# Hybrid decoder step on one core: row splits, memory queries, W_out scaling and the loads of expert chunks 3 to 5 in another order

## What is computed

```
z = rmsnorm(x) @ w_in                     # 1024 -> 1792
q, k, v, cb, cc, cv, mq = split(z)
attn  = sliding-window attention, 8 heads, 2 kv heads, sinks, ALiBi
conv  = cb * short causal conv of (cc * cv)
cross = attention of mq over 256 memory tokens, 4 heads
mix   = groupnorm_concat([attn, conv, cross]) * g_mix
h     = x + mix @ w_out
y     = h + MoE(rmsnorm(h))               # top 4 of 32 experts, clamped SwiGLU, d_ff 1024
out   = rmsnorm(y)
mk, mv = split(rmsnorm(mem_prompt) @ w_mem_kv)
```

## Time and profile before

| | |
|---|---|
| median of 3 runs | 1434.65 us (1434.53 to 1435.76) |
| the profiled execution | 1433.95 us, of which span 1432.2 us |
| PE busy | 1392.0 us, 97% of the span |
| DVE busy | 1206.6 us, 84% |
| ACT busy | 1009.8 us, 71% |
| POOL busy | 399.3 us, 28% |
| moved by DMA | 461.97 MB, mean 323 GB/s |

### The profile page before, as it was taken

How to read it: one execution, slowest core, us unless ns; L and a number is a source line. 1 busy time by engine, 2 the same in 40 slices (tenths; PEclk the granted TensorE clock), 3 DMA queues, 4 the chain that set the end, 5 groups by cost and what they waited for, 6 DMA issues and landing times.

```text
span 1432.2 us, 18899 instructions
## 1 busy us (share of the span) xinstructions
PE 1392.0 (97%) x6899; PEld 1025.1 (72%) x6899; DVE 1206.6 (84%) x1100; ACT 1009.8 (71%) x973; POOL 399.3 (28%) x231
## 2 busy tenths in 40 slices
PE   7999999899999999999999999999999999999995
PEld 4987754677777777777777777777777777777773
DVE  5465555699999999999999999999999999999996
ACT  5345422587777777777777777777777777777774
POOL 2012211334455664222222222222222222222203
PEclk9999999799999999999999999999999999999998
DMA  9520363699999998999999999999999999999984
GB/s 329 229 64 16 137 254 126 220 378 359 374 374 373 364 362 342 374 386 379 360 391 370 371 370 362 370 368 362 372 363 368 371 367 364 373 372 367 364 309 146
DMA packets 52374, 461.97 MB, mean 323 GB/s; under 512 B 11481, under 2 KB 15547, under 8 KB 26601
## 3 DMA queue, kind: packets, MB, share of 16 engines
q1 hardware_dynamic: 40041, 439.11, 79.2%
q0 software_dynamic: 10624, 20.42, 6.5%
q10 hardware_dynamic: 1648, 1.65, 0.4%
HBM read 447.41 MB, written 24.31 MB: 329 GB/s over the span
## 4 chain that ended last, share of the span: by engine, by line
PE 91%; DVE 2%; ACT 2%; DMA 2%; issue 1%; POOL 1%; SPq 0%; POOLq 0%; ACTq 0%; DVEq 0%
PE psum L2365 25%; PE psum L2366 24%; PE psum L2367 24%; PE psum L2135 4%; PE psum L2378 2%; PE psum L1973 2%; PE psum L1975 2%; PE psum L1974 2%; PE psum L2349 2%; PE psum L2360 2%; DMA ring<-in_x_prompt 1%; ACT ring L908 1%; PE psum L1940 1%; DMA hn_tbl<-area 1%; POOL small L806 0%
## 5 line engine op out<-in xcount | busy, mean ns | idle before, releaser
L1697 DVE TENSOR_TENSOR low<-raw,high 128x2048 fp32r<-128x2048 f32 x384 | 865.2, 2283 | 43.4 <-ACT high L1094 42.6
L1094 ACT CAST high<-raw 128x2048 fp32r<-128x2048 f32 x384 | 725.1, 1913 | 97.5 <-PE psum L2367 88.8
L2365 PE MATMUL psum<-high,area_r 128*104 128x512 f32 x1536 | 610.8, 398 | 0.9 <-DVE area_r L1768 0.9
L2366 PE MATMUL psum<-high,area_r 128*104 128x512 f32 x1536 | 603.7, 393 | 0.0
L2367 PE MATMUL psum<-low,area_r 128*104 128x512 f32 x1536 | 602.8, 392 | 0.0
L2367 PEld LDWEIGHTS psum<-low,area_r 128*104 128x104 f32 x1536 | 257.9, 168 | 97.2
L2365 PEld LDWEIGHTS psum<-high,area_r 128*104 128x104 f32 x1536 | 258.0, 168 | 91.8 <-DVE area_r L1768 1.3
L2366 PEld LDWEIGHTS psum<-high,area_r 128*104 128x104 f32 x1536 | 258.4, 168 | 90.5
L724 POOL DMA_INDIRECT area<-hn_tbl,idx_i x32 | 158.4, 4949 | 100.1 <-DVE idx_i L1664 71.4
L689 POOL CAST pick_r<-area 64x104 fp32r (+1 forms) x33 | 30.8, 933 | 460.2 <-PE psum L2367 449.6
L737 POOL DMA_INDIRECT y_tbl<-area,idx_i x31 | 61.8, 1995 | 222.9 <-ACT area L1104 199.7
(11 more groups left out here) (288 smaller groups left out, 1189.3 us busy)
## 6 DMA issues: line engine op xcount, KB each, us to landing
raw<-in_w_gate_up SPq DMA_DIRECT2D x128, 2048.0 KB, 10.9
raw<-in_w_down SPq DMA_DIRECT2D x64, 2048.0 KB, 11.1
ring<-in_w_in SPq DMA_DIRECT2D x7, 1024.0 KB, 15.3
ring<-in_x_prompt SPq DMA_DIRECT2D x8, 512.0 KB, 10.0
ring<-in_w_out SPq DMA_DIRECT2D x7, 512.0 KB, 4.5
ring<-in_w_mem_kv SPq DMA_DIRECT2D x2, 1024.0 KB, 9.3
ring<-in_mem_kT SPq DMA_DIRECT2D x1, 2048.0 KB, 8.6
ring<-in_cache_mem_v SPq DMA_DIRECT2D x1, 2048.0 KB, 8.2
```

Source lines behind the costliest of these rows:

```text
L1094: nc.scalar.copy(high_w(i), raw_w(t)).then_inc(sem("w_high"), 1)
L1697: v.tensor_tensor(low_w(t), raw_w(t), high_w(i), ALU.subtract).then_inc(sem("w_low"), 1)
L2365: mm(bank, high, wh, start=start, stop=False)
L2366: mm(bank, low, wh, start=False, stop=False)
```

## The change

The same instructions run, in another order, and some waits are set elsewhere:

- SP loads chunks 3 and 4 of the first expert not before the last row block's stores but together with chunk 5, after the first gather.
- ACT splits x tiles 2 and 3 ahead of the first weights; it does not wait for the first memory product there. It evicts the first projection tile before it waits for the low bias parts, and copies the memory's keys three tiles' work later.
- DVE does x_low(2) and x_low(3) before the first weights' low part, and subtracts the biases behind the eviction of the first projection tile.
- `mq_diagonals` moves from ahead of the scores of unit 2 to behind those of unit 4; tile 6 of W_out is scaled ahead of 4 and 5, and PE waits for each group of tiles by itself.
- DVE waits for the last stores of the normalised rows only in the branch for overflowing experts.

```diff
@@ SP @@
-                if j == NTT - 1:
-                    sp.wait_ge(sem("group_pe"), 2)
-                    load_chunk(0, 3)
-                    load_chunk(0, 4)
                 sp.wait_ge(sem("h_part"), 6 * (j + 1) if j < 4 else 26)
...
             sp.wait_ge(sem("gathered"), 16)
-            load_chunk(0, 5)
+            sp.wait_ge(sem("group_pe"), 2)
+            for q in range(3, 6):
+                load_chunk(0, q)
             sp.wait_ge(sem("route_ready"), 1)
@@ ACT @@
             ac.wait_ge(sem("ss_ready"), 7)
-            ac.wait_ge(sem("mkv_pe"), 1)
-            w_split(0)
             x_split(2)
             x_split(3)
+            ac.wait_ge(sem("xT_pe"), 4)
+            w_split(0)
             mem_out(0)
...
-            ac.wait_ge(sem("bias_low"), 1)
-            w_split(2)
-            ac.wait_ge(sem("mkv_pe"), 3)
-            nc.scalar.copy(view(ring, 7424, [512]), banks[4][:, :]).then_inc(sem("mkT_ready"), 1)
...
                 nc.scalar.copy(z_out(t, 1), banks[7][:, 0:HALF]).then_inc(sem("z_act"), 1)
+                if i == 0:
+                    ac.wait_ge(sem("bias_low"), 1)
+                    w_split(2)
                 if i + 3 < NZ:
                     w_split(i + 3)
...
             for t in (8, 0, 1, 2, 3):
                 z_odd(t)
+                if t == 0:
+                    ac.wait_ge(sem("mkv_pe"), 3)
+                    nc.scalar.copy(view(ring, 7424, [512]), banks[4][:, :]).then_inc(sem("mkT_ready"), 1)
@@ DVE @@
+            x_low(2)
             norm(6)
+            x_low(3)
             w_low(0)
-            x_low(2)
             rows_T(4)
-            x_low(3)
+            x_low(4)
             rows_T(5)
-            x_low(4)
             rows_T(6)
             x_low(5)
             x_low(6)
             w_low(1)
-            dv.wait_ge(sem("bias_high"), 1)
...
                 v.tensor_copy(z_out(t, 0), banks[6][:, 0:HALF]).then_inc(sem("z_dve"), 1)
+                if i == 0:
+                    dv.wait_ge(sem("bias_high"), 1)
...
             denominators(1, 1)
-            mq_diagonals()
             scores(2)
...
             scores(4)
+            mq_diagonals()
             denominators(4)
...
-            for t in range(3, 7):
+            for t in (3, 6, 4, 5):
                 gain(t)
...
-            for par, n in ((0, 3), (1, 2)):
-                dv.wait_ge(sem(f"st_hn{par}"), 16 * n)
             link(v.tensor_copy(cnt, banks[0][:, 160:192]))
...
             with dv.If(flag > 0):
 
+                for par, n in ((0, 3), (1, 2)):
+                    dv.wait_ge(sem(f"st_hn{par}"), 16 * n)
@@ PE @@
-            pe.wait_ge(sem("wo_ready"), 1 + KD)
+            pe.wait_ge(sem("wo_ready"), 6)
             pe.wait_ge(sem("exp_ready"), HB[8])
             part(0, 0)
...
             probs_T(8, (0, 1))
+            pe.wait_ge(sem("wo_ready"), 7)
             part(0, 1)
...
             pe.wait_ge(sem("ulr_ready"), 1)
+            pe.wait_ge(sem("wo_ready"), 1 + KD)
             part(0, 2)
```

More of the change, by code:

```diff
@@ L1315, in _ @@
             w_low(1)
-            dv.wait_ge(sem("bias_high"), 1)
-            v.tensor_tensor(bias_r[2 * NE:3 * NE, 2 * D:3 * D], bias_raw[2 * NE:3 * NE, 2 * D:3 * D],
-                            bias_r[2 * NE:3 * NE, 2 * D:3 * D], ALU.subtract)
-            v.tensor_tensor(bias_r[NE:2 * NE, 0:2 * D], bias_raw[NE:2 * NE, 0:2 * D], bias_r[NE:2 * NE, 0:2 * D],
-                            ALU.subtract).then_inc(sem("bias_low"), 1)
             def z_even(t):
@@ L1326, in z_even @@
                 v.tensor_copy(z_out(t, 0), banks[6][:, 0:HALF]).then_inc(sem("z_dve"), 1)
+                if i == 0:
+                    dv.wait_ge(sem("bias_high"), 1)
+                    v.tensor_tensor(bias_r[2 * NE:3 * NE, 2 * D:3 * D], bias_raw[2 * NE:3 * NE, 2 * D:3 * D],
+                                    bias_r[2 * NE:3 * NE, 2 * D:3 * D], ALU.subtract)
+                    v.tensor_tensor(bias_r[NE:2 * NE, 0:2 * D], bias_raw[NE:2 * NE, 0:2 * D], bias_r[NE:2 * NE, 0:2 * D],
+                                    ALU.subtract).then_inc(sem("bias_low"), 1)
                 if i + 2 < NZ:
```

## The result

| | before | after |
|---|---|---|
| median | 1434.59 us (1431.37 to 1435.76, 4 runs) | 1420.76 us (1420.56 to 1421.88, 4 runs) |
| the profiled execution | 1433.95, span 1432.2 | 1420.56, span 1418.7 |
| PE busy | 1392.0 us | 1388.6 us |

The ratio is 0.9909, with a 95% interval of 0.9892 to 0.9926: faster by 13.8 us. The forecast was 1422.0, range 1418.5 to 1427.5.

The account below looks back on a forecast made before the run. The prediction took the chain of waits in the first 270 us, mostly through PE with few gaps, as the bound. Its terms, 3.7 + 3.8 + 0.1 + 5.3 = 12.9 us, took the median 1434.65 to 1421.75, said as 1422; range 1418.5 to 1427.5.

Parts of the forecast that it names:

- Term 1: Start of the input projection: evicting the first half tile before the low bias parts removes gap and half clock; 3.7 us.
- the row order: Row splits ahead of the first projection tile: eviction of rows 4 at nearly the same time; gain 0.2 us, bounds 0 to 0.7.
- Term 2: Memory queries moved from ahead of unit 2's scores: shorter PE idling and no clock fall; 3.8 us, bounds 2.5 to 3.9.
- Term 3: Waits for W_out: PE starts 1.6 us earlier but waits longer before unit 9's probabilities; 0.1 us, bounds 0 to 1.6.
- Term 4: Loads ahead of the last store: without chunks in front it lands earlier; 5.3 us, bounds 3.0 to 5.5.
- PE's clock does ahead of the first expert what it did before: Assumption for the stretch before the first expert: the clock's behaviour stays the same, moved with the earlier start.
- The price of the loads: Three chunks in flight when the experts begin delay refills, but 1 to 2 us are left; cost taken as nothing.
- rival (a): Loads crowd the second gather; PE would wait 2.2 us and could lose clock: 1424 to 1426 us; chance 0.17.
- a PE wait for a gather: Sign that the prediction is wrong, listed beside ACT casts waiting for chunks and a later clock drop; no size given.
- Rival (c): Expert stage paced by its loads, once landings exceed about 21 us and stay there: slower, 1441 us; chance 0.04.
- Rival (b): Gains at the projection start and memory queries partly taken up further on, by clock or another engine: 1424.5 to 1426; chance 0.15.
- (d): W_out is worth its full 1.6 us and the clock returns earlier before the first expert: 1419 to 1420.5; chance 0.06.

Follow-up runs that it names:

- e9_norm_first: The changed kernel with only the scaling of rows 6, norm(6), moved ahead of x_low(2) on DVE; 1420.06 us, ratio 0.9899.
- e5_rows_old: The changed kernel with the row splits and first weight split back in the old order on ACT and DVE; 1420.83 us, ratio 0.9911.
- e3_wo: The kernel before with only the W_out part: tile 6 scaled ahead of 4 and 5, PE's wait split in three; 1434.59 us, ratio 1.0001.
- e4_loads: The kernel before with only chunks 3 to 5 loaded behind the first gather and DVE's store wait in the overflow branch; 1430.48 us, ratio 0.9968.
- e12_change_again: The changed kernel itself, unaltered, timed again beside the last group of variants; 1420.71 us, ratio 0.9899.
- e6: The changed kernel with norm(6) ahead of x_low(2) and the eviction of rows 4 ahead of w_low(0) on DVE; 1417.70 us, ratio 0.9887.
- e10: The changed kernel with only the eviction of rows 4 moved ahead of w_low(0) on DVE; 1419.11 us, ratio 0.9889.
- e11: The changed kernel with both DVE moves, norm(6) and the eviction of rows 4, run a second time; 1418.97 us, ratio 0.9889.
- e1_bias: The kernel before with only the DVE and ACT order around the first projection tile changed, row splits left old; 1430.83 us, ratio 0.9973.
- e2_mq: The kernel before with only mq_diagonals moved from ahead of unit 2's scores to behind unit 4's; 1427.84 us, ratio 0.9957.
- e8_mq_gap: The kernel before with mq_diagonals moved between the two denominators of unit 1 on DVE; 1430.08 us, ratio 0.9976.

## Why the prediction was right, and where not

**Term 1**, predicted 3.7, came out at 3.4: the scores of unit 0 moved from 68.93 to 65.53. The gap of 2.20 and the half clock behind it went as forecast, with no new wait for the third tile's weights; from the memory's keys to the scores of unit 0 it took 25.24 us for 29.03, so this part gave 3.8 where 3.5 was forecast. The step that failed is the row order, taken as a gain of 0.2: PE's gap ahead of rows 6 grew from 3.12 to 3.43, and rows 6 came 0.38 later (28.07 to 28.45). "DVE's eviction of rows 4 has one more x split ahead of it, started about a split's length earlier, so it comes at nearly the same time" took the earlier start for as much as the added split. The split takes 1.14 us, and what it fills are the 0.73 us for which DVE had waited for ACT ahead of w_low(0), so the eviction comes 0.39 later (27.03 for 26.64). POOL's power, slower beside x_low(2) (2.12 us for 0.99), is not the cause: e9_norm_first has it back at 0.99 with the same gap. Without the 0.38 term 1 is 3.8. That e5_rows_old has the change's time within 0.1 us says that the row order as made is worth nothing either way by the medians.

**Term 2**, predicted 3.8, was 4.0: the scores of unit 4 on DVE moved by 7.40 us (123.79 to 116.39), 3.4 of them term 1's. PE idles 0.62 us at unit 2's second transposes, and the clock holds. The delay behind the scores of unit 4, an estimated 1.4 us, was 0.25: the group took only 1.26 us there, without a wait for POOL, and it fills the 1.09 us for which DVE had waited for ACT before. From the start of these scores to conv(0) it is 4.09 us for 3.84. It cost nothing.

**Term 3**, predicted 0.1, was 0.2 in the change and in e3_wo. The new wait for POOL is there, 0.75 + 0.43 = 1.2 us in two pieces where one of 1.6 was forecast; ACT's 0.46 at 163 takes the rest.

**Term 4**, predicted 5.3, was 5.5 in the change and 5.75 in e4_loads, from the issue of the last store to the transposes. "PE's clock does ahead of the first expert what it did before" did not hold. In the change's profile the clock fell already in 240:245, so that the gather's index became the last thing that it waited for, not the store; and it was back sooner, 1.1 us to the good. In e12_change_again, the same kernel, it was not: from the transposes to the first refill it took 10.4 us (252.46 to 262.83), against 8.9 in the change's first profile (252.76 to 261.61) and 10.0 in before (265.84 to 275.83). PE's first transposes and the refill in e12_change_again:

```profile
252.46 1.65 PE L2352 MATMUL psum<-cst,area 104*128 104x104 f32 x8 [2.84 <-DMA area<-hn_tbl,idx_i]
...
262.83 19.42 SPq L456 DMA_DIRECT2D raw<-in_w_gate_up  x4
```

Yet the 1.1 is not mere chance of one execution. In six of the fourteen profiles PE has no idle time right ahead of the transposes (the change, e5, e6, e9, e10 and e11), since its spare matmuls ran at the lower level until the gather had landed; there the stretch takes 8.3 to 8.9 us. In the other eight PE idles there for 2.8 to 9.6 us, and it takes 9.6 to 11.0. All six have the new loads together with terms 1 to 3, and e12_change_again is the one of the seven profiles of that kind (the change twice, and five with its row splits in another order) that doesn't go that way; its profile is also the slowest of its four runs. So the whole change mostly brings this gain, and e4_loads alone (10.95) didn't. What makes the clock fall early, in 240 to 250 us, stays open.

**The price of the loads**, predicted as nothing, was 0.8: rival (a), in small. The prediction had named a PE wait for a gather as a sign of being wrong, and it came, not at the second gather, for which the margin was reckoned, but at the next (317.81 for transposes that would have run at 317.25), which took 21.6 us: 0.56 us. The other 0.3 show in no wait. All eight profiles with the new loads have this wait, 0.24 to 1.20 us. But the old loads don't exclude it. Of the six profiles that issue chunks 3 and 4 ahead of the gather two have it, e3_wo with 0.23 and e1_bias with

```profile
330.03 0.93 PE L2352 MATMUL psum<-cst,area 104*128 104x104 f32 x8 [1.23 <-DMA area<-hn_tbl,idx_i]
```

The longest gather up to 520 us took 21.2 to 22.2 us with the new loads, 19.5 to 22.2 with the old. So the new order makes the wait regular, and not all of the 0.8 is its own. No clock was lost with it. Rival (c), an expert stage paced by its loads, did not come: chunks issued in 255 to 420 landed in up to 18.5 us (15.6 before), not 21 and more, and no cast waited. Rival (b) did not come either, and of (d) only the clock half.

The sum is 3.4 + 4.0 + 0.2 + 5.5 + 1.1 - 0.8 = 13.4 us, against 13.4 between the two profiled executions (1433.95 and 1420.56) and 13.8 between the medians. The forecast of 12.9 was right in the mechanism of its three large parts. That the total fits so closely is luck: its misses (row order -0.6, price -0.8, clock +1.1, the rest +0.8) nearly cancel.

The best version of this study is the change with the eviction of rows 4 ahead of w_low(0) and norm(6) at the front: 1417.70 and 1418.97 us in two groups of runs, 1.7 to 3.1 under the change, of which the rows show 1.25 without the clock's part.

## What to carry to other kernels

When work is put ahead of something on an engine, count all that then stands ahead of the piece that another engine waits for, and follow each producer of it; the sign of a half-microsecond term can turn on one operation. Ahead of an indirect gather on the critical path hold large loads back, those of another engine's queue too: here that was worth 8.5 us. A wait removed from PE is a gain only if the chain that PE meets next was not already as late; look there first.

## What the runs showed of the hardware that I had not expected

- The same gap does not always bring the clock down. Behind the 2.2 us ahead of the second tile the granted clock in 41 to 46 us was 0.66 in before's profile, 0.69 in e3_wo's and 0.71 in e4_loads', and 1.00 in e2_mq's and e8_mq_gap's. That is some 1.3 us between two executions of one stretch of code. The runs of before spread over 5.9 us (1431.02 to 1436.88); how much of that is the clock, no run tells. So the effects of single parts, taken by medians, need not add up to that of the whole. What decides it in an execution stays open.
- Small operations are held up by a large one on the neighbouring engine: POOL's power on 32x1 took 2.12 us in place of 0.99 beside a DVE subtraction of 128x1024, DVE's copy of 64x32 up to 1.44 in place of 0.18 beside POOL's product of 128x1024. Neither appears as a wait.
- The first indirect gather of 104 rows took 4.66 to 5.29 us in the kernels that had no chunk in flight ahead of it (4.98 in before), 11.96 behind two chunks of 2 MB, and among the experts gathers took up to 22.2.
